# Even attention: stack copies issued ahead of modulation weights, one modulation product moved to the output projection, index sums in score order

## The chip, the cores and the metric

The kernel runs on one core of a Trainium2 chip. The metric is device time in microseconds (us) of one execution: the median of a few runs. The engines are TensorE (PE, matrix products), VectorE (DVE), ScalarE (ACT), GpSimd (POOL) and SyncE (SP, whose queue issues most DMA transfers). Each has its own instruction stream; they meet through semaphores.

## The reference, cut to what matters

All matrices are float32; the token count is 512, the width 1024, a second sequence ("context") has 256 tokens. A first block does two attentions, one of which keeps, for every query, the 128 keys with the best index score:

```python
dots  = einsum('bqhd,bsd->bqhs', qi_blk, ki)                 # 8 index heads
score = einsum('bqhs,bqh->bqs', relu(dots), wi_blk)          # summed over heads
_, sel = lax.top_k(where(causal, score, -inf), topk)         # topk = 128
```

A second block has two layers. Each is modulated by vectors made of a conditioning row:

```python
mod_x = silu(c) @ w_mod[l] + b_mod[l]        # w_mod[l] is 1024 x 3072; the same for the context
sh, sc, g = split(mod_x, 3)
h  = rms_norm(x, norm_pre[l]) * (1 + sc) + sh
mx, mc = mixer(h @ w_in, hc @ w_in, ...)     # layer 0: "even", layer 1: "odd"
x  = x + g * rms_norm(mx @ w_out[l], norm_post[l])
```

The even mixer is a differential attention (8 heads, two softmax maps each: `a = p[:, :, 0] - lam * p[:, :, 1]`), own queries over context and own keys, context queries over context keys, beside a short convolution `b * conv(c * u)`.

## The kernel before, in words

**Precision.** Every large product is done in three passes: an operand x is split in a rounded high part (cast by ACT) and a low part x - high (subtracted by DVE or POOL), and PE adds high*high, high*low and low*high in float32.

**The weight stream.** All weights lie in one array of "granules" of 1 MB, in the order in which PE wants them. A w granule holds four "units" of 128 rows x 512 columns; an m granule holds half of one modulation product's weights. SP fetches the granules in order (line 1412) into the two slots of `w_raw`, granule g into slot g mod 2. Before it issues granule g it waits until granule g-2 is used up: a w granule when ACT has cast (line 1436) and POOL has subtracted (line 1255) its four units, an m granule when PE has multiplied straight out of the slot. SP's queue is strictly in order, so whatever stands ahead of a granule delays it.

**Modulation products.** There are twelve, (layer, i) with i from 0 to 5. Six are "guests" of a host gemm (`GUEST`): `modulate` does one half after unit 1 and the other after unit 5 of the host (line 772). The other six, (0,4), (0,5), (1,0), (1,1), (1,2) and (1,3), are done whole inside the loop of the even attention (`modulate_whole`, `MOD_AFTER`: after steps 2, 10, 18, 26, 34, 42). The row that comes out is copied by ACT (`guest_rows`, line 1491); for i < 4 a small product turns it into columns (`turn_row`, line 754, two steps later or in `turn_due`) for DVE.

**The even attention's loop.** `EVEN` has 48 steps, 12 for each of four head pairs: 4 with context queries, then 8 with own queries; even steps belong to the pair's first head, odd ones to its second. A step's scores (`score_even`, line 1040) multiply a query stack and a key stack of 96 rows: for a head and map, the parts high, high, low of the keys beside high, low, high of the queries, 32 rows each. These stacks are put together by small SBUF-to-SBUF copies that SP issues (`stacked`, line 1317): 6 for a head's keys, 6 for its queries. `stacks(step)` issues them in five lots: -1 (heads 0 and 1, 24 copies), 1 (head 2), 10 (head 3), 13 (heads 4 and 5), 23 (heads 6 and 7); a lot s >= 0 waits for the scores of step s. Between scores PE transposes the step before last but one (line 1048), multiplies with the values (line 1064), and does the pieces of the convolution's products (`slim`, line 688; `FEED_E`), whose weights are six w granules. DVE takes the maxima (line 2550), ACT the exponentials (line 1826), POOL and DVE scale.

**Where the lots stand in SP's queue** is planned when the program is made: the loop over granules puts a lot ahead of granule g once g is at least that of unit cb_1's last (line 1378) and the lot's step is below the step at which granule g-2 comes free (`freed_in`, line 1372). That gives, in the loop: granules (0,4) half 0, (0,4) half 1, lots -1 and 1, w bb_0/cb_1, (0,5) half 0, (0,5) half 1, w ub_1/bb_1, (1,0) half 0, lots 10 and 13, (1,0) half 1, w cb_2/ub_2, (1,1) half 0, lot 23, (1,1) half 1, w bb_2/cb_3, and so on. `even_units` is the last unit that ACT and POOL may split at a step.

**After the loop:** gemms gc and e_ga, then the output projection: eo0 (8 units, the first 512 output columns, own tokens), eo1 by token tiles (`by_tiles`, line 796), then both for the context, transposes of the new x, gemm n_q of the odd layer with the context's transposes in its midst (`turn_context`, line 826), gemm n_k. ACT's stream holds its casts of weight units (`high(...)`) between its other work by hand.

**The index stage**, early in the kernel: PE scores the 24 items of `INDEX` (pair, tile t = 1..3, head of the pair) in blocks of four over four PSUM banks (line 838, function `score_pair`), each bank reused in the next block. ACT applies relu (line 1582) and DVE sums (lines 2268, 2271), in the order `INDEX_SUMS` (line 437). DVE then runs 16 rounds of the top-k search (lines 2337 and 2340), with the gates of `ga` (line 2299) after round 8.

Of the kernel before, what the change touches and what calls it, by code (L numbers as in the profile page):

```python
# [56 lines left out]

NARROW = ("ma0", "ma1", "ma2", "ma3", "gn0", "gn1", "gd0", "gd1")
# [8 lines left out]
LATE_HOSTS = ("n_k", "ud")  # L67
EVEN_MODS = [m for m in MODS if m not in MODS[:4] + MODS[10:]]
GUEST = {host: mod for host, mod in zip(HOSTS + LATE_HOSTS, MODS[:4] + MODS[10:])}
# [9 lines left out]
for _b in range(N_UNITS // 4):  # L79
# [5 lines left out]
    if 0 <= _j < len(EVEN_MODS):  # L85
        GRANULES += [("m", EVEN_MODS[_j], half) for half in range(2)]
# [164 lines left out]
def build(nc, dram, out):  # L251

    with ExitStack() as ctx:  # L253
# [183 lines left out]
        INDEX_SUMS = [6 * pr + n for pr in range(HEADS // 2) for n in (0, 2, 1, 3, 4, 5)]  # L437
# [16 lines left out]
        MOD_AFTER = {GRANULE_STEPS * j + 2: mod for j, mod in enumerate(EVEN_MODS)}  # L454
        TURN_AFTER = {step + 2: mod for step, mod in MOD_AFTER.items() if mod[1] < 4}

        def even_units(s):

            granules_in = (s - 5) // GRANULE_STEPS + 1
            return min(fed["e"][2 * s - 1] + ROOM, UNITS[SLIM[0]][0] + 4 * granules_in + 3)  # L460
# [124 lines left out]
        def _(pe):  # L585
# [178 lines left out]
            def gemm(chunk, x, c=None, ready=None, midway=None, part="xc"):  # L764
# [3 lines left out]
                for k in range(n):  # L768
# [3 lines left out]
                    if chunk in GUEST and k in (1, 5):  # L772
                        modulate(*GUEST[chunk], int(k > 1))
# [352 lines left out]
            by_tiles("eo1", mixed, gives_back=False)  # L1126
# [179 lines left out]
        def _(sp):  # L1306
# [65 lines left out]
            def freed_in(granule):  # L1372
                if granule[0] == "w":
                    return split_in(4 * granule[1] + 3)
                return min([s for s, mod in MOD_AFTER.items() if mod == granule[1]], default=len(EVEN))

            for g in range(N_GRANULES):
                if g >= granule_of(UNITS["cb_1"][-1]):
# [45 lines left out]
        def _(act):  # L1424
# [147 lines left out]
            for n, i in enumerate(INDEX_SUMS):  # L1572
                pr, t, hh = INDEX[i]
                w = P * (t + 1)
                if n % 6 == 0 and pr + 1 < HEADS // 2:
                    prep_i(pr + 1)
# [353 lines left out]
            mixed_out(0, range(ST))  # L1930

# [36 lines left out]
            high(UNITS["n_k"][1])  # L1968
# [134 lines left out]
        def _(dve):  # L2103
# [156 lines left out]
            for n, i in enumerate(INDEX_SUMS):  # L2260
                pr, t, hh = INDEX[i]
                h, w = 2 * pr + hh, P * (t + 1)
                if n % 6 == 0 and pr + 1 < HEADS // 2:
                    prep_i(pr + 1)
# [36 lines left out]
            def scale_up(layer):  # L2301
                a, b = COL[f"npre{layer}"]
                link(dve.scalar_tensor_tensor(MC[:, layer, 8:16, :], MC[:, layer, 8:16, :], 1.0,
                                              COLS[:, a:b].unsqueeze(2).broadcast_to((P, 8, 2)), ALU.add, ALU.mult))

            def modulation(layer, parts, rows=None):
# [17 lines left out]
                if 3 in parts:  # L2324
                    for i in (2, 3):
                        consumed(dve, ("modT", layer, i))
                    scale_up(layer)
# [6 lines left out]
            for n in range(TOPK // 8):  # L2334
# [6 lines left out]
                if n == 8:  # L2341
                    gated("ga", GA)
# [295 lines left out]
            for i in range(4):  # L2638
                consumed(dve, ("modT", 1, i))
            shifts = COLS[:, COL["bmod1"][0]:COL["bmod1"][0] + 16].unsqueeze(2).broadcast_to((P, 16, 2))  # L2640
# [149 lines left out]
```

## Time and profile before

Median 1315.1 us of 3 runs (1314.51 to 1316.66).

| | |
|---|---|
| profiled execution | 1319.82 us, its span 1317.9 us, mean granted TensorE clock 0.981 |
| PE | 1246.1 us busy (95%) |
| PE weight loads | 999.3 us (76%) |
| DVE | 675.4 us (51%) |
| ACT | 632.7 us (48%) |
| POOL | 463.3 us (35%) |
| DMA | 140.33 MB, mean 106 GB/s |

PE matmuls overlap one another: a 512-column matmul is shown as 0.39 us but the next one starts 0.23 us after it. An idle time is counted from the end so shown. The bar of PE in 40 slices of 33 us, with the granted clock under it:

```
PE   7999999999999999899598989999999999999997
PEclk9999999999999999999798989999999999999999
```

The dips in slices 19, 21 and 23 (counted from 0) lie in the even attention's loop, which runs from 649 to 877 us.

### The profile page before, as it was taken

Reading aid. Unit: us, or ns where it says so; the run is one execution under the profiler, and the core shown is the slowest. Engines: PE = TensorE matmul, PEld = TensorE weight load, DVE = VectorE, ACT = ScalarE, POOL = GpSimd, SP = SyncE. Lnnn points to the kernel's source line nnn. Section 1 sums busy time; section 2 is a strip of 40 time slices with the busy share of each in tenths; the row PEclk is TensorE's granted clock in tenths of the full one; section 3 lists DMA queues with packets and bytes.
Section 4 is the critical chain, followed back from the end, with each engine's and each line's share of the span. In section 5 each row is a group of like instructions: output and inputs, shape, how many; then the busy total and the mean of one; then the engine's idle time right before and its main releaser. Section 6 shows DMA issues by size and latency. Waiting matters only on the chain. (4 is left out here: it accounts for less than half of the span.)

```text
span 1317.9 us, 19569 instructions
## 1 busy us (share of the span) xinstructions
PE 1246.1 (95%) x7148; PEld 999.3 (76%) x7148; DVE 675.4 (51%) x1293; ACT 632.7 (48%) x1355; POOL 463.3 (35%) x360
## 2 busy tenths in 40 slices
PE   7999999999999999899598989999999999999997
PEld 6877777776788788888476767788878788777785
DVE  4676966655315245547173637551834701555353
ACT  7544327654523366623264646552546422655533
POOL 5544434221444455512132323331452323222351
PEclk9999999999999999999798989999999999999999
DMA  6322541101322523501325341221234232221442
GB/s 230 134 72 70 187 160 65 65 33 49 128 97 95 193 96 106 197 1 65 113 94 182 116 168 59 93 75 65 96 112 146 85 115 86 67 94 65 161 133 91
DMA packets 28429, 140.33 MB, mean 106 GB/s; under 512 B 4304, under 2 KB 5712, under 8 KB 15728
## 3 DMA queue, kind: packets, MB, share of 16 engines
q1 hardware_dynamic: 21584, 117.72, 25.5%
q10 hardware_dynamic: 6752, 21.35, 4.9%
q8 instruction: 60, 0.98, 0.3%
q14 instruction: 33, 0.27, 0.1%
HBM read 122.74 MB, written 6.29 MB: 98 GB/s over the span
## 5 line engine op out<-in xcount | busy, mean ns | idle before, releaser
L1255 POOL TENSOR_TENSOR w_low<-w_raw,w_high 128x512 fp32r<-128x512 f32 x256 | 350.5, 1381 | 653.0 <-ACT w_high L1436 652.4
L1436 ACT CAST w_high<-w_raw 128x512 fp32r<-128x512 f32 x256 | 153.9, 621 | 258.5 <-PE psum L660 171.7
L660 PE MATMUL psum<-x_high,w_high 128*128 128x512 f32 x528 | 219.2, 415 | 3.7 <-DVE e_conv L2614 1.0
L660 PE MATMUL psum<-x_high,w_low 128*128 128x512 f32 x528 | 206.6, 391 | 0.0
L660 PE MATMUL psum<-x_low,w_high 128*128 128x512 f32 x528 | 206.2, 391 | 0.0
L660 PEld LDWEIGHTS psum<-x_high,w_high 128*128 128x128 f32 x528 | 99.7, 189 | 32.8 <-issue 10.1
L660 PEld LDWEIGHTS psum<-x_high,w_low 128*128 128x128 f32 x528 | 99.1, 188 | 21.6
L660 PEld LDWEIGHTS psum<-x_low,w_high 128*128 128x128 f32 x528 | 99.6, 189 | 16.6 <-issue 1.0
L2550 DVE TENSOR_REDUCE small<-psum 128x1 f32<-128x768 f32 (+1 forms) x96 | 70.0, 771 | 72.1 <-PE psum L1040 72.1
L660 PE MATMUL psum<-w_high,x_high 128*128 128x512 f32 x224 | 88.4, 395 | 0.9 <-POOL w_low L1255 0.6
L660 PE MATMUL psum<-w_high,x_low 128*128 128x512 f32 x224 | 87.3, 390 | 0.0
L660 PE MATMUL psum<-w_low,x_high 128*128 128x512 f32 x224 | 87.2, 389 | 0.0
L1284 POOL TENSOR_SCALAR arena<-arena,small 128x768 f32<-128x768 f32 (+1 forms) x48 | 40.3, 840 | 124.3 <-DVE small L2557 124.3
L1826 ACT ACTIVATE arena<-psum,small 128x768 f32<-128x768 f32 (+1 forms) x84 | 63.2, 759 | 32.4 <-DVE small L2550 32.0
L1835 ACT COPY arena<-psum 128x512 f32<-128x512 f32 (+1 forms) x80 | 36.7, 459 | 72.8 <-PE psum L1048 72.3
L660 PEld LDWEIGHTS psum<-w_high,x_high 128*128 128x128 f32 x224 | 42.1, 188 | 13.8 <-issue 4.2
L660 PEld LDWEIGHTS psum<-w_high,x_low 128*128 128x128 f32 x224 | 42.0, 188 | 8.9
L660 PEld LDWEIGHTS psum<-w_low,x_high 128*128 128x128 f32 x224 | 42.1, 188 | 8.4
L1040 PE MATMUL psum<-b_both,q_masked 96*128 96x512 f32 (+1 forms) x100 | 25.2, 358 | 21.8 <-issue 20.3
L688 PE MATMUL psum<-x_high,w_high 128*128 128x512 f32 x96 | 43.5, 454 | 0.0
L2562 DVE SCALAR_TENSOR_TENSOR arena<-arena,small 128x768 f32<-128x768 f32 (+1 forms) x36 | 30.1, 835 | 20.7 <-POOL arena L1284 20.6
L1040 PEld LDWEIGHTS psum<-b_both,q_masked 96*128 96x128 f32 x100 | 16.6, 198 | 30.4 <-issue 26.7
(484 smaller groups left out, 2862.0 us busy)
## 6 DMA issues: line engine op xcount, KB each, us to landing
w_raw<-stream SPq DMA_DIRECT2D x98, 1024.0 KB, 4.9
x_kept<-arena ACTq DMA_DIRECT2D x8, 512.0 KB, 3.7
arena<-x_kept ACTq DMA_DIRECT2D x8, 512.0 KB, 5.6
arena<-bias ACTq DMA_DIRECT2D x8, 512.0 KB, 3.9
q_masked<-e_q_high SPq DMA_DIRECT2D x24, 96.0 KB, 2.5
arena<-x SPq DMA_DIRECT2D x4, 512.0 KB, 5.2
arena<-x ACTq DMA_DIRECT2D x4, 512.0 KB, 5.0
arena<-ctx ACTq DMA_DIRECT2D x4, 512.0 KB, 4.4
```

Of the source, the lines that this page charges most:

```text
L660: mm = pe.matmul(o, l, r, start=(first and n == 0 and kind != "fc"), stop=(last and n == len(passes) - 1))
L688: mm = pe.matmul(o, l, r, start=k == 0 and n == 0, stop=k == NK - 1 and n == 2)
L1040: mm = pe.matmul(acc[:, c0:c1], q, k[:, c0:c1], start=True, stop=True)
L1255: pool.tensor_tensor(PLACE[u][1], RAW[:, g % 2, u % 4, :], PLACE[u][0].bitcast(F32), ALU.subtract).then_inc(w_lo, 1)
L1284: pool.tensor_scalar(second, second, SM[:, RINV + c + 1:RINV + c + 2], SM[:, 82:83], ALU.mult, ALU.mult)\
L1436: act.copy(PLACE[u][0], RAW[:, g % 2, u % 4, :]).then_inc(w_hi, 1)
L1826: frees(act.activation(map_place(s, m), PS[:, 512 * b:512 * b + w], ACT.Exp, bias=scr(NEGMAX + c), accum_out=scr(ROWSUM + c)), key)
L1835: frees(act.copy(E_PT[:, 2 * (d % 2) + hh, P * c:P * c + w], ps[:, 0:w]), key)
L2550: dve.tensor_reduce(scr(NEGMAX + 2 * (s % 4) + m), PS[:, 512 * b:512 * b + w], AX.X, ALU.max, negate=True).then_inc(sig("e_neg"), 1)
L2562: dve.scalar_tensor_tensor(e0, e0, scr(RINV + c), e1, ALU.mult, ALU.add).then_inc(sig("e_p"), 1)
```

## The change

Six edits, all in the order of work; what is computed stays the same.

1. SP's lots of stack copies may stand ahead of any granule after the one of cb_0 (line 1378), and an m granule counts as freed one step later than before (`freed_in`). The order in SP's queue becomes: w cb_0/ub_0, **lot -1**, (0,4) half 0, (0,4) half 1, **lot 1**, w bb_0/cb_1, (0,5) half 0, (0,5) half 1, **lot 10**, w ub_1/bb_1, (1,0) half 0, **lot 13**, (1,0) half 1, w cb_2/ub_2, w bb_2/cb_3, **lot 23**, (1,1) half 0, (1,1) half 1, w ub_3/bb_3, (1,2) half 0, (1,2) half 1.
2. The loop holds five products, after steps 2, 10, 18, 34 and 42: (0,4), (0,5), (1,0), (1,1), (1,2). None is done after step 26.
3. (1,3) becomes a guest of eo0, with its halves after units 1 and 4. Its granules stand in the stream behind the two w granules of eo0. ACT copies its row behind eo0's four tiles, PE turns it after the first token tile of eo1 (through `turn_due`), and DVE adds bias and scale then, ahead of the x3 loop.
4. eo1's tiles take the PSUM bank after turn_due's (order 0, [1], 2, 6, 4).
5. The index sums run 0, 2, 1, 3 in every block of four, as the scores do; `gated("ga")` comes after round 7 of the top-k search and not after round 8.
6. ACT no longer casts units n_k 0 and 1 between the two norms of the context (line 1968); `high(UNITS["n_k"][3])` behind the second norm casts all four.

```diff
@@ -55,6 +55,8 @@
 
 MODS = [(l, i) for l in range(2) for i in range(6)]
 
+GUEST_AT = {"eo0": (1, 4)}
+
 NARROW = ("ma0", "ma1", "ma2", "ma3", "gn0", "gn1", "gd0", "gd1")
 
 COLUMNS = 64
@@ -64,9 +66,9 @@
 
 SLIM = tuple(f"{part}_{j}" for j in range(4) for part in ("cb", "ub", "bb"))
 HOSTS = ("ga", "gb", "vb", "mb0")
-LATE_HOSTS = ("n_k", "ud")
-EVEN_MODS = [m for m in MODS if m not in MODS[:4] + MODS[10:]]
-GUEST = {host: mod for host, mod in zip(HOSTS + LATE_HOSTS, MODS[:4] + MODS[10:])}
+LATE_HOSTS = ("eo0", "n_k", "ud")
+EVEN_MODS = dict(zip((0, 1, 2, 4, 5), MODS[4:9]))
+GUEST = {host: mod for host, mod in zip(HOSTS + LATE_HOSTS, MODS[:4] + MODS[9:])}
 UNITS = {}
 _n = 0
 for _name, _k in STREAM:
@@ -82,7 +84,7 @@
         if 4 * _b in UNITS[_name]:
             GRANULES.append(("m", _mod, UNITS[_name].index(4 * _b) // 4))
     _j, _rest = divmod(4 * _b - UNITS[SLIM[0]][0], 4)
-    if 0 <= _j < len(EVEN_MODS):
+    if _j in EVEN_MODS:
         GRANULES += [("m", EVEN_MODS[_j], half) for half in range(2)]
 N_GRANULES = len(GRANULES)
 GRANULE = {g: n for n, g in enumerate(GRANULES)}
@@ -434,7 +436,7 @@
 
 
         INDEX = [(pr, t, hh) for pr in range(HEADS // 2) for t in range(1, ST) for hh in range(2)]
-        INDEX_SUMS = [6 * pr + n for pr in range(HEADS // 2) for n in (0, 2, 1, 3, 4, 5)]
+        INDEX_SUMS = [first + n for first in range(0, len(INDEX), 4) for n in (0, 2, 1, 3)]
 
 
         BOTH = [(name, i) for name in "ab" for i in range(ATT[name].steps)]
@@ -451,13 +453,14 @@
         FEED_E = ((2, 1), (2, 1), (2, 2), (3, 3))
 
         GRANULE_STEPS = 8
-        MOD_AFTER = {GRANULE_STEPS * j + 2: mod for j, mod in enumerate(EVEN_MODS)}
+        MOD_AFTER = {GRANULE_STEPS * j + 2: mod for j, mod in EVEN_MODS.items()}
         TURN_AFTER = {step + 2: mod for step, mod in MOD_AFTER.items() if mod[1] < 4}
 
         def even_units(s):
 
-            granules_in = (s - 5) // GRANULE_STEPS + 1
-            return min(fed["e"][2 * s - 1] + ROOM, UNITS[SLIM[0]][0] + 4 * granules_in + 3)
+            in_step, rest = divmod(s - 5, GRANULE_STEPS)
+            known = in_step + 1 if in_step in EVEN_MODS or in_step < 0 else in_step + 2
+            return min(fed["e"][2 * s - 1] + ROOM, UNITS[SLIM[0]][0] + 4 * known + 3)
 
         N_CONSTS = 3
 
@@ -769,7 +772,7 @@
                     if ready:
                         ready(k)
                     unit(chunk, k, x, c, part)
-                    if chunk in GUEST and k in (1, 5):
+                    if chunk in GUEST and k in GUEST_AT.get(chunk, (1, 5)):
                         modulate(*GUEST[chunk], int(k > 1))
                     if k == min(3, n - 2):
                         turn_due()
@@ -1123,7 +1126,7 @@
             pool[0] = (3, 7, 4, 5, 6)
             gemm("eo0", mixed, mixed_c, ready=lambda k: pe.wait_ge(sig("mix_lo"), 3 * (k // 2) + 3), part="x")
             pool[0] = (0, 1, 2, 6, 4)
-            by_tiles("eo1", mixed, gives_back=False)
+            by_tiles("eo1", mixed, lambda t: turn_due(), gives_back=False)
             pool[0] = (3, 7)
             for k in range(NK):
                 unit("eo0", k, mixed, mixed_c, "c")
@@ -1372,10 +1375,10 @@
             def freed_in(granule):
                 if granule[0] == "w":
                     return split_in(4 * granule[1] + 3)
-                return min([s for s, mod in MOD_AFTER.items() if mod == granule[1]], default=len(EVEN))
+                return min([s + 1 for s, mod in MOD_AFTER.items() if mod == granule[1]], default=len(EVEN))
 
             for g in range(N_GRANULES):
-                if g >= granule_of(UNITS["cb_1"][-1]):
+                if g > granule_of(UNITS["cb_0"][-1]):
                     while made < len(STACK_STEPS) and STACK_STEPS[made] < freed_in(GRANULES[g - 2]):
                         stacks(STACK_STEPS[made])
                         made += 1
@@ -1572,8 +1575,8 @@
             for n, i in enumerate(INDEX_SUMS):
                 pr, t, hh = INDEX[i]
                 w = P * (t + 1)
-                if n % 6 == 0 and pr + 1 < HEADS // 2:
-                    prep_i(pr + 1)
+                if n % 6 == 0 and n // 6 + 1 < HEADS // 2:
+                    prep_i(n // 6 + 1)
                 if n >= 3:
                     high(fed["i"][n - 3] + ROOM)
                 ps = filled(act, ("i", i))
@@ -1928,6 +1931,7 @@
 
             high(UNITS["eo1"][-1])
             mixed_out(0, range(ST))
+            guest_rows(GUEST["eo0"])
 
             def e_ready(t):
                 consumed(act, ("eo0", t))
@@ -1965,7 +1969,6 @@
                 act.wait_ge(sig("x3"), ST + t + 1)
 
             rms("eo_c", LT, lambda t: E_O[:, ST + t, :], context_out, M_JUNK, c=ST)
-            high(UNITS["n_k"][1])
             rms("x3_c", LT, lambda t: E_O[:, ST + t, :], context_summed, M_JUNK, c=ST, each=True)
             high(UNITS["n_k"][3])
             affine_pairs("c3T")
@@ -2260,8 +2263,8 @@
             for n, i in enumerate(INDEX_SUMS):
                 pr, t, hh = INDEX[i]
                 h, w = 2 * pr + hh, P * (t + 1)
-                if n % 6 == 0 and pr + 1 < HEADS // 2:
-                    prep_i(pr + 1)
+                if n % 6 == 0 and n // 6 + 1 < HEADS // 2:
+                    prep_i(n // 6 + 1)
                 consumed(dve, ("i", i))
                 r, acc = A_R[:, n % 2, 0:w], A_SC[:, t - 1, 0:w]
                 if h == 0:
@@ -2297,11 +2300,6 @@
                 for j in range(4):
                     dve.wait_ge(sig(f"{c}_sig"), j + 1)
                     frees(dve.tensor_tensor(g[:, j, :], g[:, j, :], BANK[fills[(c, j)][0]][:, :], ALU.mult), (c, j))
-
-            def scale_up(layer):
-                a, b = COL[f"npre{layer}"]
-                link(dve.scalar_tensor_tensor(MC[:, layer, 8:16, :], MC[:, layer, 8:16, :], 1.0,
-                                              COLS[:, a:b].unsqueeze(2).broadcast_to((P, 8, 2)), ALU.add, ALU.mult))
 
             def modulation(layer, parts, rows=None):
                 for i in parts:
@@ -2324,7 +2322,9 @@
                 if 3 in parts:
                     for i in (2, 3):
                         consumed(dve, ("modT", layer, i))
-                    scale_up(layer)
+                    a, b = COL[f"npre{layer}"]
+                    link(dve.scalar_tensor_tensor(MC[:, layer, 8:16, :], MC[:, layer, 8:16, :], 1.0,
+                                                  COLS[:, a:b].unsqueeze(2).broadcast_to((P, 8, 2)), ALU.add, ALU.mult))
 
             link(dve.tensor_scalar(A_MASK[:, 0:P], square("causal"), -1.0, None, ALU.mult))
             tiles = [(t, P * (t + 1), A_SC[:, t - 1, 0:P * (t + 1)], A_SCW[:, t - 1, 0:P * (t + 1)],
@@ -2338,7 +2338,7 @@
                 for t, w, sc, work, best in tiles:
                     tile_ready(t)
                     turn_of(t, dve.match_replace(work, best, work if n else sc, TAKEN))
-                if n == 8:
+                if n == 7:
                     gated("ga", GA)
                 if n == 12:
                     modulation(0, (0,))
@@ -2635,11 +2635,11 @@
             dve.wait_ge(sig("subln"), 6)
             gates("e_ga", "e_ga_g", values)
             low_mixed([XL[:, j, :] for j in range(4)] + ctx_of(CL), [XH[:, j, :] for j in range(4)] + ctx_of(CH), values, 6)
-            for i in range(4):
+            for i in range(3):
                 consumed(dve, ("modT", 1, i))
-            shifts = COLS[:, COL["bmod1"][0]:COL["bmod1"][0] + 16].unsqueeze(2).broadcast_to((P, 16, 2))
-            link(dve.tensor_tensor(MC[:, 1, :, :], MC[:, 1, :, :], shifts, ALU.add))
-            scale_up(1)
+            biases = COLS[:, COL["bmod1"][0]:COL["bmod1"][0] + 12].unsqueeze(2).broadcast_to((P, 12, 2))
+            link(dve.tensor_tensor(MC[:, 1, 0:12, :], MC[:, 1, 0:12, :], biases, ALU.add))
+            modulation(1, (3,))
             dve.wait_ge(sig("row0"), 4)
 
             def x3_normed(t):
```

## Rows read from the trace of the kernel before

**Rows 1.** PE's waits: who waited for whom; us in total, times, longest.
```profile
PE psum L1040 <- issue: 20.3, 3, 13.0
PE psum L745 <- DMA w_raw<-stream: 7.0, 3, 5.8
```
**Rows 2.** Timeline of PE: start, us, line, op, out<-in, count [idle before].
```profile
648.78 0.55 PE L1040 MATMUL psum<-b_both,q_masked 96*128 96x256 f32 x1 [13.02 <-issue]
...
663.60 0.51 PE L1040 MATMUL psum<-b_both,q_masked 96*128 96x256 f32 x2
```
**Rows 3.** Timeline of SP's queue, 638 to 699.
```profile
638.26 0.54 SPq L1317 DMA_DIRECT2D b_both<-k_high  x1
...
652.87 0.59 SPq L1317 DMA_DIRECT2D q_masked<-e_q_high  x1
...
698.99 0.47 SPq L1317 DMA_DIRECT2D b_both<-k_high  x1
```
**Rows 4.** DMA issues by line: count, KB each, median us from issue to landing.
```profile
w_raw<-stream SPq DMA_DIRECT2D x98, 1024.0 KB, 4.9
...
q_masked<-e_q_high SPq DMA_DIRECT2D x24, 96.0 KB, 2.5
```
**Rows 5.** Timeline of DVE ahead of the loop.
```profile
608.38 1.79 DVE L2159 TENSOR_TENSOR k_low<-arena,k_high 128x512 fp32r<-128x512 f32 x1
```
**Rows 6.** Timeline of PE: scores of steps 10, 12, 14, 24, 26.
```profile
693.08 0.39 PE L1040 MATMUL psum<-b_both,q_masked 96*128 96x512 f32 x1
...
703.77 0.28 PE L1040 MATMUL psum<-k_high,b_both 96*128 96x256 f32 x1
...
719.22 0.28 PE L1040 MATMUL psum<-k_high,b_both 96*128 96x256 f32 x1
...
761.99 0.40 PE L1040 MATMUL psum<-b_both,q_masked 96*128 96x256 f32 x2
...
769.63 0.41 PE L1040 MATMUL psum<-b_both,q_masked 96*128 96x256 f32 x2
```
**Rows 7.** Timeline of PE: scores of steps 29, 38, 41.
```profile
791.65 0.60 PE L1040 MATMUL psum<-k_high 96*128 96x512 f32 x2
...
834.60 0.28 PE L1040 MATMUL psum<-k_high,b_both 96*128 96x256 f32 x1
...
844.89 1.02 PE L1040 MATMUL psum<-b_both,q_masked 96*128 96x512 f32 x3
```
**Rows 8.** Timeline of PE: index stage, then the guests in gb and vb.
```profile
89.96 0.73 PE L838 MATMUL psum<-b_high,q_masked 64*128 64x512 f32 x4 [1.46 <-ACT arena L1582]
...
157.79 1.06 PE L730 MATMUL psum<-w_raw,mod_x 128*32 128x512 f32 x8 [1.06 <-DVE gate_a L2299]
...
164.36 0.95 PE L754 MATMUL psum<-sel_sb,mod_rows 128*128 128x2 f32 x8
...
183.22 1.06 PE L730 MATMUL psum<-w_raw,mod_x 128*32 128x512 f32 x8 [0.21 <-DVE gate_b L2299]
```
**Rows 9.** Timelines of PE, SP and POOL around eo1.
```profile
981.75 0.62 PE L796 MATMUL psum<-q_masked,b_high 128*128 128x512 f32 x2
...
988.31 0.62 PE L796 MATMUL psum<-q_masked,b_high 128*128 128x512 f32 x2
...
975.38 0.33 SPq L1412 DMA_DIRECT2D w_raw<-stream  x1
...
982.36 5.03 POOL L1255 TENSOR_TENSOR x_low<-w_raw,x_high 128x512 fp32r<-128x512 f32 x4 [2.07 <-ACT x_high L1436]
```
**Rows 10.** Timelines of DVE, POOL and PE at the odd layer's start.
```profile
992.18 1.29 DVE L2140 SCALAR_TENSOR_TENSOR arena<-arena,small 128x1024 f32<-128x1024 f32 x1
...
1041.25 3.67 POOL L1255 TENSOR_TENSOR w_low<-w_raw,w_high 128x512 fp32r<-128x512 f32 x2 [15.85 <-ACT w_high L1436]
...
1041.66 4.34 DVE L2154 SCALAR_TENSOR_TENSOR arena<-arena,small 128x1024 f32<-128x1024 f32 x2
...
1048.55 3.62 PE L826 MATMUL psum<-squares_sb,arena 128*128 128x128 f32 x16 [2.08 <-DVE arena L2483]
```

## The prediction

> **What bounds the kernel now.** I read the bar of PE in 40 slices first. It is full but for the first and last slice and for dips in slices 19, 21 and 23, so time is won where PE stands still, and hardly elsewhere. The list of PE's waits comes next: the largest sum is at the score line L1040 with "issue" as its end, 20.3 us in three times, and the next of this region is 5.8 us at L745 for weights [rows 1]. "Issue" at L1040 means that the profile names no engine: what the scores wait for are SP's stack copies. Third, PE's timeline at the loop's start: its last product of e_v ends at 648.78 - 13.02 = 635.76, and the first scores start at 648.78 [rows 2]. Fourth, SP's queue: the first copy of lot -1 is issued at 638.26, the 24th at 652.87, that is one in 0.64 us [rows 3], and one lands 2.5 us after its issue [rows 4]. The first head has 12 copies: 638.26 + 12 x 0.64 + 2.5 = 648.4. So the start of the loop is set by the place of lot -1 behind two modulation granules, the second of which waits until ACT and POOL have split cb_0/ub_0, beside PE's last units of e_v.
>
> The sum is made against the profiled execution, 1319.8 us, whose span is 1317.9. It is 4.7 us above the median of the runs, 1315.1; I take the same distance for the changed kernel.
>
> **Loop start (edit 1).** Lot -1 now needs the first key tile's low part, which DVE makes at 608.38 to 610.2 [rows 5], and no longer the split of cb_0/ub_0. 24 copies of 0.64 us end at 625.5 and have landed by 628, 8 us before PE ends e_v. The two granules behind it lose nothing: half 0 of (0,4) is issued at 625.5, half 1 waits for the split of ub_0 as before (637.8) and lands, by the 4.9 us of rows 4, at 642.7 or a little later. PE's three steps up to step 3 are then 10 pieces of convolution products, 3 x 0.23 us each and two of them half as wide (6.4 us), three scores of 0.4, and one product at 2 x 1.06 [rows 8]: 9.7 us, so step 3 starts at 635.8 + 9.7 = 645.5 and not at 663.60 [rows 2]. That is 18.1 us less: 13 of waiting, 2.3 of a second wait before step 1, and the rest the half clock that follows them. Bounds: by the length of two context steps of a running pair, 769.63 - 761.99 = 7.6 us for two [rows 6], the three steps and the product would take 13.6, a gain of 14; the most is 19.
>
> **Head 3 (edit 1).** Lot 10 is issued at 698.99 [rows 3], behind two granules that wait for the product after step 10; its last copy lands too late for step 13. From step 12 to step 14 PE takes 719.22 - 703.77 = 15.45 us, and the same two steps of the next pair 7.64 [rows 6]: 7.8 us are to be had. In the new order the lot goes out when step 10's scores are done, 693.08 + 0.9 = 694.0 [rows 6]; 12 copies need 7.7 to 9 us, landing 2.5: 704.2 to 705.5. Step 13 without a wait would start at 703.77 + 3 = 706.8. It fits, by 1.3 us at the least. Granule ub_1/bb_1 now goes out behind the lot, some 6 us later than before; its first unit is cast in step 13, just after it has landed. I take 7.8, and bounds of 4 and 7.8.
>
> **Product (1,1) out of step 26 (edit 2).** Its second half waits 5.8 us for a granule that stands behind lot 23 and behind the split of cb_2/ub_2. From step 26 to 29 PE takes 791.65 - 769.63 = 22.02 us; the same steps of the last pair, without product and turn, 844.89 - 834.60 = 10.29 [rows 6, 7]. 11.7 us less, of which 3.1 are work that comes back at eo0. In the new order the granules of (1,1) go out behind lot 23 too, but are wanted after step 34 only, half a pair later. ub_3/bb_3 waits for half 0 of a product after step 34, as before. Bounds 9 and 11.7.
>
> **eo0 and eo1 (edits 3, 4).** The guest costs PE 1.06 us a half, and the turn 0.95 [rows 8]: 3.1 us. The row is copied by ACT and turned behind eo1's first tile, DVE's added wait is over before the sum of squares of that tile; what is queued behind it (the x3 loop) needs this tile first. The stream is what gets late. eo1's first block now waits in `w_raw` for the split of eo0's second (975.3 by POOL's pace, where it used to go out at 950), and eo1's last block for half 1 of the guest, which PE does after unit 4, at about 975.4; it was issued at 975.38 before [rows 9], so the last block is not later, but both 1 MB blocks now travel together and POOL must subtract eight units in a row behind the first landing, 980.3: at 5.03 / 4 = 1.26 us each [rows 9] the eighth is done at 991.0. PE reaches eo1 at 981.75 + 2.1 = 983.9 and would need 24 x 0.23 = 5.4 us for the tile; it ends it at 991.7, 7.8 us later, where it took 988.31 - 981.75 = 6.6 [rows 9]. That is 1.2 us more. Together +4.3; bounds +3.1 (cover holds) and +8 (the last block lands 3 us later, with the half clock after it). The x3 chain of ACT and DVE starts with the tiles of eo1 and shifts with PE.
>
> **Casts of n_k (edit 6).** The two casts release two subtractions on POOL, 3.67 us for two where POOL needs 1.26 each elsewhere, and in the same stretch DVE's two sums take 4.34 us where one takes 1.29 alone [rows 9, 10]. Without POOL beside them DVE ends 1.8 us sooner, and PE's 2.08 us of waiting at the context's transposes shrinks to about 0.5; these 16 transposes run at half clock (3.6 us) and would take half. That is 3.3 us less. All four subtractions then fall beside DVE's next chain (the context's affine part), which ends 1.1 us ahead of n_k now: I give back 0.6. -2.7, bounds -3.8 and +1.
>
> A rule bears on this and in part against it. The Trainium skill (GPSIMD Engine Reference, Key points) says that POOL shares its SBUF interfaces with VectorE and contends with DVE instructions that have two SBUF inputs. Rows 10 agree, on both engines. By that rule the contention is moved rather than removed: DVE's four subtractions with two SBUF inputs in the affine part are now met by all four of POOL's.
>
> **Index sums (edit 5).** PE waits twice for 1.46 us on relu, in the third and the sixth block, since item 7 (or 19) is taken behind an item of the next block while the next block's bank waits for it [rows 8] (the row of the first; the second is alike, at 118.41). In the new order no item is behind one of a later block: -2.9, bounds 0 and -3. What follows (kb, DVE's search) starts from PE's end of kb and shifts with it. The gates a round earlier remove 1.06 us at 157.79, but PE then comes to the next place that DVE's same stream sets, gate_b at 183.22, where it waits 0.21 already [rows 8], and waits there for it: 0, bounds -1 and +1.
>
> **Sum:** -18.1 - 7.8 - 11.7 + 4.3 - 2.7 - 2.9 = -38.9. 1319.8 - 38.9 = 1280.9 as profiled; 1276.2 for the median. Ends of the bounds: -47 and -16, which will not all fall on one side.
>
> **Rivals.** *A, the waits come back in part:* with head 3 on time, DVE and ACT have less slack; PE already waits 1.4 us on an exponential at steps 9 and 33, each with half clock behind it, and such a wait may appear in the second pair too; head 3 may miss its 1.3 us. That gives back 4 to 7.8 us, and the eo1 bound 3.7: 1281 to 1288. For it: the margin is small. Against it: the last pair, with every lot landed long before, runs with no wait of this kind. *B, better than the sum:* the waits at steps 9 and 33 go as well (3 us each with the clock) and eo1 is covered: 1268 to 1272. Against it: nothing in DVE's work of those steps changes. *C, the change doesn't do what it says:* lot -1 stays behind something in SP's queue (the low keys or queries, or a transfer ahead) until near 636: the loop's start keeps 10 to 14 us of its wait: 1287 to 1291. Against it: SP stands waiting without a transfer from 621.5 to 637.8. *D, slower than before:* lots ahead of w granules starve the splits. The price of one granule that PE must wait for is that of step 26, 11.7 - 3.1 = 8.6 us. Five granules go out behind a lot or in another order (bb_0, ub_1, (1,0) half 1, (1,1), cb_2/ub_3); if all five stop PE, 43 us are lost: 1276 + 43 = 1319. It decides from the fifth on. Against it: each has 3 us or more of slack by the steps above.
>
> **How the numbers follow.** Forecast with its own range, 1272 to 1281: 0.58. A 0.22, B 0.10, C 0.07, D 0.03. The range of 1268 to 1289 takes in A and B. A change under 0.2% (2.6 us) can't be told from none in this kernel. Every case but D is faster: faster 0.96, same 0.01, slower 0.03.
>
> **What would show it.** Right: the first scores directly behind e_v with no idle time over 0.5 us; no "issue" wait at L1040; no wait over 1 us at L745; a granted clock of 1.0 from 636 to the first wait at step 9; a step 12 to step 14 distance of about 7.6 us and a step 26 to step 29 distance of about 10.3; PE waiting on POOL for the last four units of eo1's first tile; two sums of DVE in 2.6 us before the context's transposes; no wait in the index stage over 0.5 us, and a longer wait for gate_b. Wrong: stack copies at 638 or later, waits on raw weights of the splits in the loop, or PE waiting at eo1 for a transfer for more than 3 us.

## The result, and the profile after

| | median of the runs | profiled execution | its span | mean granted clock |
|---|---|---|---|---|
| before | 1315.88 us (1314.51 to 1318.56) | 1319.8 us | 1317.9 us | 0.98 |
| changed | 1281.28 us (1277.34 to 1282.17) | 1282.1 us | 1280.3 us | 0.995 |

The ratio is 0.9721, with a 95% interval of 0.9700 to 0.9743. The profiled execution is 37.7 us shorter, where the sum said 38.9. The median is 5.1 us above the forecast of 1276.2, inside the range and 0.3 us above the upper end of the likeliest case's own range.

PE's waits in the changed kernel (who waited for whom; us in total, times, longest): "issue" at the score line, 20.3 us before [rows 1], is gone, and the product line waits 1.1 us in all, where it waited 7.0.

```profile
PE psum L1043 <- ACT arena L1829: 2.9, 2, 1.5
...
PE psum L819 <- DVE merge_a L2489: 2.2, 1, 2.2
...
PE psum L799 <- POOL x_low L1258: 1.2, 4, 0.3
...
PE psum L748 <- DMA w_raw<-stream: 1.1, 2, 0.6
```

SP's queue: the 24 copies of lot -1 now begin at 607.68, the last goes out at 623.07, and the two transfers behind it are the halves of product (0,4). The last copy of lot 10 goes out at 680.10. Before, its first copy was issued at 698.99 [rows 3].

```profile
607.68 1.17 SPq L1320 DMA_DIRECT2D b_both<-k_high  x2
...
623.07 0.59 SPq L1320 DMA_DIRECT2D q_masked<-e_q_high  x1
623.76 11.90 SPq L1415 DMA_DIRECT2D w_raw<-stream  x2
...
680.10 0.59 SPq L1320 DMA_DIRECT2D q_masked<-e_q_high  x1
```

The last matmul of e_v (first line), then PE's scores of steps 0, 3, 9, 12, 14, 26, 29 and 33 (start, duration, [idle before]). They answer to rows 2, 6 and 7: the first scores stand directly behind e_v; step 0 to 3 takes 9.8 us, step 12 to 14 7.65, step 26 to 29 10.29. Two waits for an exponential are left, at steps 9 and 33.

```profile
632.84 0.39 PE L663 MATMUL psum<-w_high,ctx_low 128*128 128x512 f32 x1
633.06 0.40 PE L1043 MATMUL psum<-b_both,q_masked 96*128 96x256 f32 x2
...
642.86 0.51 PE L1043 MATMUL psum<-b_both,q_masked 96*128 96x256 f32 x2
...
665.35 1.03 PE L1043 MATMUL psum<-b_both,q_masked 96*128 96x512 f32 x3 [1.53 <-ACT arena L1829]
...
683.00 0.28 PE L1043 MATMUL psum<-k_high,b_both 96*128 96x256 f32 x1
...
690.65 0.28 PE L1043 MATMUL psum<-k_high,b_both 96*128 96x256 f32 x1
...
741.00 0.41 PE L1043 MATMUL psum<-b_both,q_masked 96*128 96x256 f32 x2
...
751.29 0.39 PE L1043 MATMUL psum<-k_high 96*128 96x512 f32 x1
...
767.96 0.47 PE L1043 MATMUL psum<-k_high 96*128 96x512 f32 x1 [1.37 <-ACT arena L1829]
```

At eo1 PE waits five times for POOL, which subtracts without a pause. The tile's first matmul, the first and the last of the five waits, and the turn of the product's row behind the tile: the tile takes 8.5 us, where it took 6.6 [rows 9].

```profile
943.60 0.62 PE L799 MATMUL psum<-q_masked,b_high 128*128 128x512 f32 x2
...
946.38 0.47 PE L799 MATMUL psum<-ctx_high,b_high 128*128 128x512 f32 x1 [0.31 <-POOL ctx_low L1258]
...
951.35 0.47 PE L799 MATMUL psum<-x_high 128*128 128x512 f32 x1 [0.30 <-POOL x_low L1258]
...
952.11 0.95 PE L757 MATMUL psum<-sel_sb,mod_rows 128*128 128x2 f32 x8
```

At the odd layer's start DVE's two sums take 2.48 us where they took 4.34, and the transposes wait 0.41 where they waited 2.08 [rows 10]. But a subtraction of DVE now takes 1.61 us instead of 0.68, beside POOL's four, and PE waits 0.93 for it at the start of n_k. DVE, then POOL, then PE:

```profile
1006.38 2.48 DVE L2157 SCALAR_TENSOR_TENSOR arena<-arena,small 128x1024 f32<-128x1024 f32 x2
...
1014.10 1.61 DVE L2162 TENSOR_TENSOR ctx_low<-tables_sb,ctx_high 128x512 fp32r<-128x512 f32 x1
...
1016.73 0.68 DVE L2162 TENSOR_TENSOR ctx_low<-tables_sb,ctx_high 128x512 fp32r<-128x512 f32 x1
```

```profile
1011.20 5.66 POOL L1258 TENSOR_TENSOR w_low<-w_raw,w_high 128x512 fp32r<-128x512 f32 x4 [21.09 <-ACT w_high L1439]
```

```profile
1011.59 1.97 PE L829 MATMUL psum<-squares_sb,arena 128*128 128x128 f32 x16 [0.41 <-DVE arena L2483]
...
1019.96 0.50 PE L663 MATMUL psum<-x_high,w_high 128*128 128x512 f32 x1 [0.93 <-DVE ctx_low L2162]
```

How far the same matmul of PE has shifted against before, stage by stage, as profiled (what the shift changes by over a stage is its term):

| stage | forecast | in this pair of profiles |
|---|---|---|
| ahead of the index stage | 0 | +0.2 |
| index sums | -2.9 | -3.4 |
| gate round | 0 | -1.1 |
| from there to the end of x2's transposes | 0 | +1.75 |
| start of the loop | -18.1 | -18.2 |
| head 3 | -7.8 | -7.8 |
| product (1,1) out | -11.7 | -11.7 |
| eo0 and eo1 | +4.3 | +4.95 |
| casts of n_k | -2.7 | -2.15 |
| behind them | 0 | -0.2 |
| all | -38.9 | -37.7 |

### The profile page after: what moved, and what is told of

Read it like the earlier page. It is cut to its first block and busy times, and to the rows that moved or that the text cites. A ratio compares the mean times of both kernels' runs of the same rounds, so it can differ in the third digit from the quotient of the medians.

```text
span 1280.3 us, 19570 instructions
## 1 busy us (share of the span) xinstructions
PE 1235.3 (96%) x7148; PEld 990.4 (77%) x7148; DVE 673.2 (53%) x1294; ACT 632.9 (49%) x1354; POOL 461.6 (36%) x360
## 5 line engine op out<-in xcount | busy, mean ns | idle before, releaser
L663 PE MATMUL psum<-x_high,w_low 128*128 128x512 f32 x528 | 206.6, 391 | 0.0
L663 PE MATMUL psum<-x_low,w_high 128*128 128x512 f32 x528 | 206.2, 391 | 0.0
L691 PE MATMUL psum<-x_high,w_low 128*128 128x512 f32 x96 | 37.8, 394 | 0.0
L691 PE MATMUL psum<-x_low,w_high 128*128 128x512 f32 x96 | 37.6, 392 | 0.0
```

The source lines that it names most:

```text
L663: mm = pe.matmul(o, l, r, start=(first and n == 0 and kind != "fc"), stop=(last and n == len(passes) - 1))
L691: mm = pe.matmul(o, l, r, start=k == 0 and n == 0, stop=k == NK - 1 and n == 2)
```

## The experiments

"Shift" is the difference in start of the same matmul of PE between two profiles; what an edit is worth is read from how the shift changes over its stage, since two profiles can already differ by up to 1 us ahead of it.

**Edit 1, half of it: the place of the lots.** The kernel before, with one line:

```
-                if g >= granule_of(UNITS["cb_1"][-1]):
+                if g > granule_of(UNITS["cb_0"][-1]):
```

> The kernel before with one condition changed: lots of stack copies may stand ahead of any granule after that of cb_0. That moves lot -1 ahead of the two halves of (0,4) and nothing else. Theory (the loop's start waits only for the place of lot -1 in SP's queue): the first scores follow e_v with under 1 us of idle time, step 3 starts 18 us sooner against e_v's end, 1298 us; head 3's wait (5 us before step 13) and the wait of the product after step 26 (5.8 us) stay. Rival (SP's queue was waiting for keys or for a transfer anyway, edit brings little alone): 1305 to 1315.

Measured: 1298.96 us, ratio 0.9863 [0.9844, 0.9881]. Against the place at which PE ends e_v the loop starts 13.2 us earlier, and step 3 comes 18.2 us earlier, as expected. Head 3's wait stays, 5.2 us in one piece:

```profile
PE psum L1040 <- issue: 5.2, 1, 5.2
```

**Edit 1 whole: `freed_in` one step later.**

```
-                return min([s for s, mod in MOD_AFTER.items() ...
+                return min([s + 1 for s, mod in MOD_AFTER.items() ...
```

> The kernel before with both halves of edit 1: lot -1 first, and an m granule counted free one step later, which puts lot 10 ahead of ub_1/bb_1. Theory: another 7.8 us below the first experiment, 1290 us; step 12 to step 14 in 7.7 us. Rival (head 3 was kept by the copies' own time, 9 us for 12, and the granule behind them comes late instead): the wait before step 13 shrinks by 2 us or less, or a wait of ACT on raw weights turns up at step 13.

Measured: 1290.87 us, ratio 0.9809 [0.9787, 0.9831]; 8.1 us less than the one before at the medians; in the profiles the first pair gains 8.2 where 7.8 was expected, and step 12 to step 14 takes 7.65 us, against 15.8 in the run before. So the threshold alone cures the loop's start, and `freed_in` on top of it head 3.

**The other edits without the lots: the product's move alone.** The changed kernel with the lots, the sums, the gate's round and the casts as before.

```
-                if g > granule_of(UNITS["cb_0"][-1]):
+                if g >= granule_of(UNITS["cb_1"][-1]):
-                return min([s + 1 for s, mod in MOD_AFTER.items() ...
+                return min([s for s, mod in MOD_AFTER.items() ...
-        INDEX_SUMS = [first + n for first in range(0, len(INDEX), 4) for n in (0, 2, 1, 3)]
+        INDEX_SUMS = [6 * pr + n for pr in range(HEADS // 2) for n in (0, 2, 1, 3, 4, 5)]
-                if n == 7:
+                if n == 8:
+            high(UNITS["n_k"][1])
```

> The changed kernel with lots, index sums, gate round and n_k casts as before: only the product (1,3) moved to eo0 and none after step 26. Theory: step 26 to step 29 takes 10.3 us and not 22.0, eo0 and eo1 cost 4.6 us more, together -7.1: 1309 us. Rival (the product's transfer was late because of the lots, so that it is late again after step 34, or the half clock moves elsewhere): a wait of several us after step 34, 1314 to 1318.

Measured: 1312.7 us, ratio 0.9964 [0.9949, 0.9979]; the profiled execution is 8.7 us shorter than that of before. Step 26 to 29 takes 10.29 us, as forecast:

```profile
770.57 0.41 PE L1043 MATMUL psum<-b_both,q_masked 96*128 96x256 f32 x2
...
780.86 0.51 PE L1043 MATMUL psum<-k_high 96*128 96x512 f32 x2
```

Against the kernel before that is the forecast's 11.7 less, and eo0 and eo1 cost 4.9; the wait after step 34 is 0.5 us. At the loop's start this run is 2.3 us behind the kernel before, although nothing is changed there: 1.7 of it is there before the loop, most of it from half clock at 551.5 that the other profile lacks, and the first scores then wait 13.62 us ("issue") and not 13.02, with half clock over that wait and what follows. Columns: the stretch, its length, busy time and instructions of PE, PEld, DVE, ACT and POOL, then the granted clock.

```profile
640.30:660.80 20.50, 8.14 (x21) 6.15 (x21) 2.24 (x7) 2.04 (x8) 1.11 (x2) 0.50 0.62 181
```

**Edit 5: the index sums back.**

```
-        INDEX_SUMS = [first + n for first in range(0, len(INDEX), 4) for n in (0, 2, 1, 3)]
+        INDEX_SUMS = [6 * pr + n for pr in range(HEADS // 2) for n in (0, 2, 1, 3, 4, 5)]
```

> The changed kernel with the index sums in the old order. Theory: PE's two waits of 1.46 us on relu in the third and sixth block are back and everything behind shifts with them, +3.1 us against the changed kernel up to the next stage (the position of the first guest of gb). Rival (the search on DVE, not PE, sets the time behind the index stage): gate_b's end keeps its place and the 3 us are absorbed.

Measured: 1283.58 us, ratio 0.9745 [0.9726, 0.9764], 2.3 us above the changed kernel's median. Over the index stage the shift grows by 3.45 us, against the changed kernel's first profile and against its second one (further below) alike; 3.1 was expected. Against the second it is still 3.45 at the end of the kernel: nothing is absorbed. Against the first, two half-clock stretches that only that one has, at 547 and 666, hide 3 us of it.

**Edit 5: the gate's round back** (`n == 7` to `n == 8`).

> The changed kernel with the gates of ga after round 8 again. Theory of the prediction (DVE's stream sets the place of gate_b, so the round brings nothing): PE waits 1.06 us for gate_a and gate_b's place does not move, 0 us. Rival (seen in the traces: DVE's first mask operation after the search took 1.34 us before and 0.31 us after, and it ends with POOL's subtraction that runs beside it; PE's earlier place moves POOL's operation out of its way): the wait for gate_a comes back, the mask operation takes 1.3 us again, gate_b and all behind it come 1.0 to 1.2 us later.

Measured: 1281.51 us, ratio 0.9729 [0.9700, 0.9757]; at the medians no difference, in the trace +1.1 over this stage. The wait for gate_a is back, 1.06 us, and that for gate_b is 0.21 against 0.28: the price moved by 0.07 and not by 1.06. What else changed is DVE's mask after the search, three operations in 2.19 us instead of 1.16. This kernel's DVE and POOL, then the changed kernel's:

```profile
177.12 2.19 DVE L2347 TENSOR_SCALAR arena<-arena 128x256 f32<-128x256 f32 x3
```

```profile
177.01 1.29 POOL L1258 TENSOR_TENSOR w_low<-w_raw,w_high 128x512 fp32r<-128x512 f32 x1
```

```profile
175.69 1.31 POOL L1258 TENSOR_TENSOR w_low<-w_raw,w_high 128x512 fp32r<-128x512 f32 x1
...
176.90 1.16 DVE L2347 TENSOR_SCALAR arena<-arena 128x256 f32<-128x256 f32 x3
```

Where the mask starts 0.11 us behind the start of a subtraction of POOL, its first operation takes 1.33 us; where POOL's subtraction ends 0.1 us after the mask's start, 0.31. This holds in all thirteen profiles: the five kernels with the gates after round 8 show 1.33 to 1.36 us there, the eight profiles with them after round 7 show 0.28 to 0.31. The Trainium skill (SBUF — State Buffer, "SBUF: two separate sides") calls the port pair of DVE and POOL an exclusive lock held for a whole instruction, against a DVE operation in a 2-port perf mode or with two SBUF inputs. The rows agree with a lock that is waited for; no run here shows in which mode this one-input operation was.

**Edit 6: the casts of n_k back.**

```
             rms("eo_c", LT, lambda t: E_O[:, ST + t, :], context_out, M_JUNK, c=ST)
+            high(UNITS["n_k"][1])
```

> The changed kernel with ACT's cast of n_k 0 and 1 back between the context's two norms. Theory (POOL's subtractions and DVE's two-input sums hold each other up): DVE's two sums take 4.3 us again and not 2.6, PE waits about 2 us at the context's transposes, +2.2 us. Rival (the cast itself, on ACT, was what delayed the second norm): DVE's sums take 2.6 us and PE waits all the same.

Measured: 1279.4 us, ratio 0.9715 [0.9691, 0.9739]: not slower than the changed kernel (0.9721 [0.9700, 0.9743]). PE's wait at the transposes is back (+1.7), but no half clock follows it and the wait at n_k's start is gone (-0.9): net +0.75 in the trace, where +2.2 was expected.

```profile
1011.51 1.97 PE L829 MATMUL psum<-squares_sb,arena 128*128 128x128 f32 x16 [2.09 <-DVE arena L2484]
```

DVE's two sums take 4.33 us again, beside POOL's two subtractions, so it is they and not the cast itself that delay the second norm:

```profile
1004.62 4.33 DVE L2158 SCALAR_TENSOR_TENSOR arena<-arena,small 128x1024 f32<-128x1024 f32 x2
```

```profile
1004.21 3.67 POOL L1258 TENSOR_TENSOR w_low<-w_raw,w_high 128x512 fp32r<-128x512 f32 x2 [15.85 <-ACT w_high L1439]
```

**The waits that are left: the convolution spread over steps.** Both waits, at steps 9 and 33, are for an exponential that waits for DVE's maximum, and DVE does three operations of the convolution (0.49, 0.75 and 0.75 us) ahead of that maximum. The changed kernel, with the three as functions in a list that the step and those behind it take from, one or two a step:

```
+            taps = []
...
-                link(dve.tensor_scalar(y, z, tap(1), None, ALU.mult))
...
+                taps.extend((middle, before, behind))
...
-                        consumed(dve, key)
-                        convolve(j, z, y, z.shape[-1])
+                        convolve(j, z, y, z.shape[-1], key)
...
+                    for _ in range(min(len(taps), 1 if (s - 1) % 12 in (6, 7) else 2)):
+                        taps.pop(0)()
```

> The changed kernel with the three operations of each convolution on DVE spread over the steps behind it, instead of all in one step. Theory (PE's waits of 1.4 us on an exponential at steps 9 and 33 come from DVE, which does a whole convolution before the next maxima; each is followed by 3.4 us of half clock): both waits and both stretches of half clock go, step 8 to step 10 takes 9.5 us and not 12.1, -5.2 us. Rival (DVE is short of time over the whole of these steps, not in one of them): the wait moves to step 10 or 11, 0 to -1 us.

Measured: 1277.32 us, ratio 0.9693 [0.9664, 0.9722], 4.0 us below the changed kernel. In the first pair and in the third PE gains 3.0 us each at the old place of the wait, half clock included; 0.6 and 0.8 of it come back later in small waits for ACT (the longest 0.65 us), so that 4.6 are left of the 5.2 expected. The score line waits 0.2 us in all:

```profile
PE psum L1043 <- ACT arena L1829: 0.2, 1, 0.2
```

**POOL's start at eo1: three casts of ACT ahead of the gates.**

```
-            high(UNITS["eo0"][3])
+            high(UNITS["eo0"][6])
             gates("e_ga", "e_ga_g", "gc_g")
...
-            high(UNITS["eo0"][0] + ROOM)
+            high(UNITS["eo0"][7])
```

> The changed kernel with ACT's casts of eo0 units 4 to 6 ahead of the gates of e_ga, where ACT stands idle for 10 us. Theory (eo1's first tile waits for POOL, which starts on eo1's eight units only when eo0's second granule has been given back): that granule is given back some 4 us sooner, PE's five waits on POOL at eo1 shrink to one or none, -1.5 us. Rival (the last granule of eo1, behind the guest's second half, sets the time; or the gates come later and PE waits in eo0): the waits stay, or go over into eo0.

Measured: 1278.9 us, ratio 0.9710 [0.9686, 0.9734]. At eo1 PE gains 0.85 us, not the 1.5 expected, and four of the five waits are left. POOL ends the eight units at 947.2 instead of 951.2, but PE comes there 3.1 us earlier too: against PE, POOL starts 0.9 us sooner. The rest by which this profile is shorter is for the most part half clock that it lacks at x2's transposes and at step 9 (3 us):

```profile
942.21 5.01 POOL L1258 TENSOR_TENSOR x_low<-w_raw,x_high 128x512 fp32r<-128x512 f32 x4
```

**The changed kernel once more, beside two variants.**

> The changed kernel as it is, timed again beside the two variants. About 1281 us, ratio 0.972 to 0.974. It serves to tell how far two profiles of one and the same kernel differ: the theory that the half-clock stretches behind waits of 1.4 to 2.3 us come and go expects shifts of up to 2 us between this trace and the earlier one of the changed kernel, each at such a stretch; the rival (they belong to the kernel) expects the same stretches at the same places.

Measured: 1280.93 us (1278.22 to 1281.06), ratio 0.9716 [0.9694, 0.9738]. The waits are the same, the clock behind them is not. Step 9 in the first profile and in this one, the wait and then the 3.4 us behind it:

```profile
665.35 1.15 PE L1043 MATMUL psum<-b_both,q_masked 96*128 96x512 f32 x4 [1.53 <-ACT arena L1829]
```

```profile
664.90:666.50 1.60, 1.15 (x6) 0.87 (x7) 1.53 (x4) 1.60 (x5) 0.00 (x0) 1.00 0.04 10
666.50:669.90 3.40, 3.40 (x28) 2.74 (x26) 3.36 (x5) 1.79 (x4) 3.20 (x3) 0.50 0.01 2
```

```profile
664.54 1.30 PE L1043 MATMUL psum<-b_both,q_masked 96*128 96x512 f32 x4 [1.36 <-ACT arena L1829]
```

```profile
665.70:669.10 3.40, 3.40 (x36) 2.81 (x34) 3.33 (x6) 1.68 (x4) 3.07 (x3) 1.00 0.02 7
```

36 matmuls against 28 in the same time. Apart from the kernel's end, the first profile has half clock at 547, 666 and 769, this one at 317, 768 and 1252. The theory of coming and going holds; where one of the two has it and the other not, the shift changes by 0.8 to 1.6 us. In both executions step 33 has it, so there the two theories can't be told apart.

**The casts of n_k, the first kept early and the fourth late.**

```
-            high(UNITS["n_k"][3])
+            high(UNITS["n_k"][0])
             affine_pairs("c3T")
+            high(UNITS["n_k"][3])
```

> The changed kernel with the cast of the first unit of n_k back ahead of the convolution's triangle, where PE meets it 0.93 us late in the changed kernel's trace, and the cast of the fourth unit moved behind the triangle. Theory: the 0.93 us wait at the start of n_k's products goes and nothing else changes, -0.9 us. Rival: VectorE's and GpSimd's subtractions fall beside other operations of each other and stretch there, or the fourth unit comes late, 0 to +1 us.

Measured: 1279.01 us, ratio 0.9710 [0.9689, 0.9732]. The line `affine_pairs` is the context's affine part, which the expectation misnames as the convolution's. The wait at n_k is gone and the transposes still wait 0.41: a shift of -0.93 there, as expected. POOL's one early subtraction (1008.97 to 1010.43) and its three late ones lie around DVE's affine part:

```profile
1008.97 1.46 POOL L1258 TENSOR_TENSOR w_low<-w_raw,w_high 128x512 fp32r<-128x512 f32 x1 [21.08 <-ACT w_high L1439]
1016.62 3.78 POOL L1258 TENSOR_TENSOR w_low<-w_raw,w_high 128x512 fp32r<-128x512 f32 x3 [6.18 <-ACT w_high L1439]
```

**All three together.**

> The changed kernel with three edits: the convolution's three VectorE operations spread over the following steps, three ScalarE casts ahead of the gates, and the n_k casts as in the variant before. The parts measured -4.8 and -2 us in the profiles (-4.0 and -2.4 us at the medians); added without overlap, with -0.9 for n_k, the sum is 1281.3 - 4.0 - 2.4 - 0.9 = 1274.0 us. But part of both medians was the absence of half-clock stretches that either removes, so the rival says 1276 to 1277 us: -2.7 and -2.4 at the two waits of the convolution, less than 1 us at eo1.

Measured: 1275.34 us (1274.82 to 1277.75), ratio 0.9679 [0.9655, 0.9703]: 5.6 us below the changed kernel timed beside it, the fastest version of all. It lies between the two expectations, 1274 and 1276 to 1277.

## Why the prediction was right, and where not

**Loop start, right.** The mechanism (lot -1's place in SP's queue) and the size (-18.1; -18.2) both stood, and the threshold alone gave the 18.2. Of them, 13.0 and 2.3 are the two waits; the rest is the half clock that followed them. The convolution's pieces add up to 6.2 us in the forecast's own terms and not to 6.4; step 0 to step 3 measured 9.8.

**Head 3, right.** Lot 10 began at 673.21, which is the forecast's 694.0 less the 20.75 us by which the loop had moved by then; its last copy, issued at 680.10, landed at 684.12, and step 13 began at 685.98. The margin was 1.9 us, the forecast said 1.3 at the least.

**Product out of step 26, right** (-11.7 by profile, and step 26 to 29 at 10.29 also when tried alone). But the size depends on the execution that it is measured against: with the product in place, step 26 to step 29 took 22.0 us before, 20.1 in the first experiment and 21.1 in the second, so that taking it out is worth 9.8 to 11.7. Alone, its net with eo0 and eo1 is only -3.6 us at the medians, against -7.1 forecast. A part of the gap is that spread and 0.3 of larger cost at eo0 and eo1; the rest stays open, since the median execution of neither kernel has a profile.

**eo0 and eo1: right in kind, 0.65 too small.** The work is 2.9 us (3.1 forecast) and the first tile of eo1 takes 2.0 us more (1.2 forecast). The experiment with the early casts shows that POOL's start sets this: POOL 0.9 us sooner against PE made PE 0.85 us faster. PE waits for five units of the tile and not for the last four.

**Index sums, right** in mechanism, 0.5 more than forecast and outside its bound of -3: the two waits are shown as 1.46 us each, counted from the modelled end of a matmul, but the start of the next one moved by 1.6 to 1.7 each time.

**Gate round: the step that failed, by 1.1 us.** "PE then comes to the next place that DVE's same stream sets ... and waits there for it: 0" assumed DVE's stream to be of fixed length. It became 1.1 us shorter (56.6 to 55.5 us from the end of kb to gate_b), since the mask no longer started under a subtraction of POOL. The experiment shows the change back with the round. The prediction weighed the contention of DVE and POOL for two-input operations, and at one place only; here it was a one-input operation at another.

**Casts of n_k: right in sign, the size mostly a matter of the execution.** The forecast -2.7 looks like the -2.15 of this pair, but 1.4 of it was half clock behind the wait in the profile of before. Of the five profiles with this wait (before, the first three experiments and that of the casts) three have half clock behind it and two don't. Without it the edit is worth 0.75 in the trace, and nothing that can be told at the medians. The give-back, 0.6 in the forecast, was 0.93. The rule weighed there (the Trainium skill, GPSIMD Engine Reference, Key points), read as contention that moves with POOL's operations, agrees with the trace. With the one early cast, which avoids both, PE is spared 0.93 us more.

**x2's transposes: +1.75 that the sum had at nothing, and that is not the change's.** PE waits 2.25 us there for DVE, where the profile of before has 1.38. It looks as if PE, earlier by the gains ahead of it, had to wait longer. But the first two experiments, in which nothing ahead of this place differs from the kernel before, wait 2.25 us as well, and so do all the others. The profile of before is the odd one: half clock from 543.4 to 546.8 stretched PE's own work ahead of the wait, and the wait shrank by as much. Before, the first experiment, the changed kernel:

```profile
549.95 0.33 PE L816 MATMUL psum<-squares_sb,merge_a 128*128 128x128 f32 x1 [1.38 <-DVE merge_a L2489]
```

```profile
543.40:546.80 3.40, 3.40 (x18) 3.40 (x18) 3.37 (x3) 0.86 (x2) 3.40 (x3) 0.50 0.01 2
```

```profile
550.66 0.33 PE L816 MATMUL psum<-squares_sb,merge_a 128*128 128x128 f32 x1 [2.25 <-DVE merge_a L2489]
```

```profile
545.84 0.33 PE L819 MATMUL psum<-squares_sb,merge_a 128*128 128x128 f32 x1 [2.25 <-DVE merge_a L2489]
```

What is left is about 1.5 us of half clock behind the wait in the changed kernel's first profile, which its second one lacks. Ahead of it two more differences cancel: a wait for POOL at 440.6 is 1.62 us and not 0.72 (0.84 to 1.86 in the other profiles), and half clock at 321.5 is in the profile of before alone of the two. Both bars of PE have a dip here that the prediction's reading of them left out (slice 16).

**Rivals.** Rival A (waits come back) didn't come in the second pair; at steps 9 and 33 the waits stayed as they were. Rival B, without them, took another edit (the convolution's). The prediction's "-47 and -16" for the ends of the bounds is a slip: its own bounds add up to about -43 and -17.

**The distance from the profile to the median: the larger error.** The forecast carried 4.7 us over from before; it was 0.8 and, the second time, 0. Behind the first 11 us, half clock lay at ten places of the profile of before, 53 us in all; after, at four, 15 us. That the distance goes with them is likely, but not shown: the median executions have no trace. Without the distance the forecast would have been 1280.9, within 0.4 us of the median; that this is so close is in part luck, since the misses of the single terms (from -1.1 to +1.75) cancel. Between the medians the change is worth 34.6 us. What remains open is why a wait of 1.4 to 2.3 us is followed by half clock in one execution and not in another.

## What to carry to other kernels

Where an in-order queue feeds the busiest engine, look for the engine's waits that have no engine as their end, and put small transfers that are ready and wanted soon ahead of large ones that must wait for a buffer anyway: two lines here gave 25 of 35 us. Count half clock behind a wait as a chance and not as a sure gain, and don't carry the distance of one profile from its median over to a kernel with other waits. Before a term under 2 us is believed, look at the same place in a second profile of the same kernel, or of one that doesn't differ up to there. Before an operation is moved, lay DVE's and POOL's rows beside each other at the old place and at the new: a place where one starts under the other can have a price, for DVE's one-input operations too.

## What the runs showed of the hardware

- An operation of DVE with one fp32 input in SBUF (128x256) took 1.33 to 1.36 us in the five profiles in which it started about 0.1 us behind the start of a POOL subtraction of 1.3 us, and ended 0.15 us behind it; in the eight others, where POOL's subtraction ended within 0.1 us of its start, it took 0.28 to 0.31.
- A subtraction of DVE with two inputs took 0.68 us alone and 1.61 beside POOL; POOL's four took 5.66 us there and 5.0 elsewhere.
- Behind a wait of 1.53 us at step 9 the granted clock was 0.50 for 3.4 us in one execution, and behind a wait of 1.36 us at the same step 1.00 in another; where only one of these two executions has such a stretch, what follows is shifted by 0.8 to 1.6 us. Where PE stood still for 13.6 us in one piece, a single stretch at 0.50 lasted 20.5 us.
